# A hybrid decoder layer on one core: another opening stage, a second exponential buffer in GLA, weight low halves in four parts

## What is computed

```python
h = rmsnorm(x, g_mix)
q_g, k_g, v_g, r_g, a_low, q_d, k_d, v_d, q_i, k_i, w_i, gate_g, gate_d = split(h @ w_in)
k_i = layernorm(k_i)
log_a = log_sigmoid(a_low @ w_gate_up + b_gate) / 16
o_g, s_new = gla_chunked(q_g, k_g, v_g, log_a, state)        # 4 heads, dk 128, dv 256
o_g = rmsnorm(o_g) * silu(r_g)
# DSA: indexer scores of 4 heads pick the top 256 causal keys of each query
score[t, s] = sum_h w_i[t, h] * relu(q_i[t, h] . k_i[s])
o_d = softmax(q_d . k_d + bias, over the picked keys) @ v_d   # 8 heads of 64
x = x + (sigmoid(gate_g) * (o_g @ w_gla) + sigmoid(gate_d) * (o_d @ w_dsa)) @ w_o
x = x + swiglu(rmsnorm(x, g_ffn));  y = rmsnorm(x, g_final)
```

## Time and profile before

| | |
|---|---|
| median of three runs | 2203.22 us (2202.76 to 2204.34) |
| profiled execution, its span | 2211.91 us, 2210.2 us |
| TensorE busy | 2096.9 us, 95% of the span |
| VectorE, ScalarE, GpSimd busy | 1072.6, 627.2, 334.7 us |
| mean granted clock of TensorE | 0.963 |

### The profile page before, as it was taken

One profiled execution on the slowest core, in us unless ns is written; L12 is line 12 of the kernel. 1 busy time (PEld: TensorE's weight loads), 2 busy tenths in 40 slices (PEclk: granted clock), 3 DMA queues, 4 the chain that ended last, 5 costly groups with the idle time before them and its releaser, 6 DMA issues. The chain is left out here.

```text
span 2210.2 us, 31133 instructions
## 1 busy us (share of the span) xinstructions
PE 2096.9 (95%) x12125; PEld 1873.6 (85%) x12125; DVE 1072.6 (49%) x2226; ACT 627.2 (28%) x1108; POOL 334.7 (15%) x294
## 2 busy tenths in 40 slices
PE   5999996999999999988889999999999999999997
PEld 4789996999999786777759987888998899889995
DVE  5489997345454330545554424444334432443245
ACT  4323221223333361444344313311212111111112
POOL 6512222333223121001013310000000000000000
PEclk7999998999999899998979999999999999999999
DMA  4202331222212242343344340211011110111002
GB/s 139 85 20 77 118 107 59 87 78 80 67 58 83 64 134 88 131 140 144 124 159 151 117 144 1 77 58 39 29 48 58 39 52 26 58 58 39 20 1 89
DMA packets 144139, 173.82 MB, mean 79 GB/s; under 512 B 9688, under 2 KB 120830, under 8 KB 143486
## 3 DMA queue, kind: packets, MB, share of 16 engines
q1 hardware_dynamic: 136158, 148.14, 20.6%
q0 software_dynamic: 7840, 23.67, 3.1%
HBM read 127.38 MB, written 44.40 MB: 78 GB/s over the span
## 5 line engine op out<-in xcount | busy, mean ns | idle before, releaser
L855 PE MATMUL ring<-n_hi,piece_hi 128*128 128x352 f32 (+1 forms) x1320 | 441.4, 334 | 1.1 <-DVE n_whole L1664 1.0
L857 PE MATMUL ring<-n_hi,piece_lo 128*128 128x352 f32 (+1 forms) x1320 | 429.5, 325 | 0.0
L856 PE MATMUL ring<-n_lo,piece_hi 128*128 128x352 f32 (+1 forms) x1320 | 429.1, 325 | 0.0
L1241 ACT ACTIVATE arena<-ring 128x352 f32<-128x352 f32 (+7 forms) x368 | 153.3, 438 | 483.6 <-PE ring L857 345.3
L2198 POOL TENSOR_TENSOR piece_lo<-piece_whole,piece_hi 128x1024 fp32r<-128x1024 f32 (+2 forms) x71 | 165.5, 2331 | 714.1 <-ACT piece_hi L1254 714.0
L855 PEld LDWEIGHTS ring<-n_hi,piece_hi 128*128 128x128 f32 (+1 forms) x1320 | 251.8, 191 | 9.0 <-issue 6.7
L856 PEld LDWEIGHTS ring<-n_lo,piece_hi 128*128 128x128 f32 (+1 forms) x1320 | 252.3, 191 | 0.6
L857 PEld LDWEIGHTS ring<-n_hi,piece_lo 128*128 128x128 f32 (+1 forms) x1320 | 251.2, 190 | 0.5
L1752 DVE TENSOR_SCALAR_CACHE_REDUCE arena<-arena 128x384 uint8<-128x384 f32 (+6 forms) x224 | 190.7, 875 | 1.4 <-DVE arena L1752 0.2
L856 PE MATMUL ring<-h_lo,gate_hi 128*128 128x352 f32 x528 | 170.7, 323 | 6.2 <-issue 6.2
L855 PE MATMUL ring<-h_hi,gate_hi 128*128 128x352 f32 x528 | 172.0, 326 | 0.0
(11 more groups left out here) (278 smaller groups left out, 3679.0 us busy)
## 6 DMA issues: line engine op xcount, KB each, us to landing
piece_whole<-w_in SPq DMA_DIRECT2D x54, 512.0 KB, 3.6
projected_rows<-arena SPq DMA_DIRECT2D x44, 528.0 KB, 2.7
arena<-projected_rows SPq DMA_DIRECT2D x12, 1056.0 KB, 5.0
gate_whole<-w_ffn_gate SPq DMA_DIRECT2D x11, 1024.0 KB, 5.2
up_whole<-w_ffn_up SPq DMA_DIRECT2D x11, 1024.0 KB, 5.3
down_whole<-w_ffn_down SPq DMA_DIRECT2D x11, 1024.0 KB, 4.7
arena<-projected_rows SPq DMA_DIRECT2D x16, 528.0 KB, 3.6
arena<-x_prompt SPq DMA_DIRECT2D x16, 512.0 KB, 5.2
```

The costliest lines, as they stand in the source:

```text
L855: pe.matmul(out, lhi, rhi, start=first, stop=False)
L856: pe.matmul(out, lhi, rlo, start=False, stop=False)
L857: return pe.matmul(out, llo, rhi, start=False, stop=last)
L1241: evacuates(act.activation(dst, src, ACT.Copy, scale=scale), *key)
```

## The change

The norm weight is laid out over all partitions (`grow`) and applied with the scaling, before the tiles are turned. The high part is copied by ScalarE and the low part subtracted by VectorE, both out of PSUM; GpSimd has no part in it. Each tile has its own buffer. The loads are issued in another order: the fourth tile stands behind the first weight loads. Six groups of pieces 0 and 1 and the page transposes run among the tiles' transposes. Pages are loaded with one DMA each instead of two, from the start on. The scores go over heads 0 and 1 of all blocks first, then 2 and 3; two groups of piece 2, the sample scores (with another order of their matmuls) and their sums are inside the list. The bias rows move behind piece 3's groups, their shift from VectorE to ScalarE. Low halves of pieces 5 to 23 are made in four instructions of 128x256. In GLA the second and fourth exponential have a buffer of their own, `eT2`, in place of `k4p`; their order in the chain changes; the next head's first difference is made before the outputs are gated, and all rows are scaled before the first is gated.

```diff
+        def early_groups(i):
+
+            return {3: [(0, 0)], 5: [(1, 0)], 6: [(0, 1)], 8: [(1, 1), (0, 2), (1, 2)]}.get(i, [])
+        def nb_after(n, g):
+            return range(4 * g, 4 * g + 4) if n == 3 and g < 2 else []
...
-        SCC = [(b, h, c0, min(512, P * (b + 1) - c0)) for b in range(2, NTP)
-               for c0 in range(0, P * (b + 1), 512) for h in range(IH)]
+        SCC = [(b, h, c0, min(512, P * (b + 1) - c0)) for f in range(2) for b in range(2, NTP)
+               for c0 in range(0, P * (b + 1), 512) for h in (2 * f, 2 * f + 1)]
+        HALF = len(SCC) // 2
+
+        def score_groups(n):
+
+            return {6: [(2, 0)], 13: [(2, 1)]}.get(n, [])
...
-        xa = [arena[:, B_kd + i * D:B_kd + (i + 1) * D] for i in range(4)]
+        xa = [arena[:, o:o + D] for o in [B_kd + i * D for i in range(4)] + [B_SC + i * D for i in range(4)] + [B_nb]]
         sqj = arena[:, B_vd:B_vd + D]
...
+        grow = arena[:, B_vd + D:B_vd + 2 * D]
...
+        eT2 = at(o_k4p, T)
...
-            sp.dma_start(arena[:, o_c128:o_c128 + n128], a["c128"]).then_inc(c_first, 16)
+            sp.dma_start(arena[:, o_c128:o_c128 + P], a["c128"][:, 0:P]).then_inc(c_first, 16)
+            load_x(0)
+            sp.dma_start(grow, a["g_mix"].to_broadcast([P, D])).then_inc(grow_in, 16)
...
+            sp.dma_start(relb[0:NB, :], a["rel_bias"]).then_inc(relb_in, 16)
+            load_x(1)
+            sp.dma_start(pagetab[0:1, :], a["page_table"].rearrange("(o b) g -> o (b g)", o=1)).then_inc(pagetab_in, 16)
+            load_x(2)
+            load(0)
+            load_x(3)
+            load_x(4)
+            load(1)
+            for i in range(5, NT):
+                load_x(i)
...
+                    for c0, cn in ((0, PAST), (PAST, DT)):
+                        for hp in range(2):
+                            for j in range(4):
+                                b = 4 * g + j
+                                rhs = kiS[:, b, :] if c0 == 0 else kiT[:, SEQ + b * DT:SEQ + (b + 1) * DT]
+                                ins = pe.matmul(ps[32 * j:32 * j + 32, c0:c0 + cn], qiS[:, 2 * b + hp, :], rhs,
+                                                start=hp == 0, stop=hp == 1)
+                    done(ins, "si", g)
...
+                for n, g in early_groups(i):
+                    if n == 0:
+                        for k in range((3 * g), min(NT, 3 * g + 3)):
+                            for c in range(2):
+                                wait_evac(pe, "h", k, c)
+                    dense(n, g)
+                    if (n, g) == (1, 1):
+                        pe.wait_ge(pg_landed, 16 * DB * NPG)
+                        for k in range(4):
+                            transposes(("ps", k), [(P * s, kpg[:, 4 * k + s, :]) for s in range(4)])
...
+            for n, (b, h, c0, w_) in enumerate(SCC):
+                for m in score_groups(n):
+                    dense(*m)
+                if n == HALF:
+                    for m in range(3):
+                        wait_evac(pe, "d", 2, m)
+                    sample_scores()
+                if n == HALF + 6:
+                    sample_sums()
...
+                    wait_full(act, "h", i, c)
+                    act.activation(n_hi[:, 4 * c:4 * c + 4, i * P:i * P + r],
+                                   bank("h", i, c).rearrange("p (a b) -> p a b", a=4)[:, :, 0:r],
...
+            square_x(0)
+            square_x(1)
+            root_x(0)
             act.wait_ge(c_first, 16 * N_FIRST)
             copy_out(vec, bank("vec")[:, 0:22], "vec")
-            for i in range(NT + 3):
...
+            square_x(2)
+            root_x(1)
+            norm_hi(0)
+            square_x(3)
+            root_x(2)
+            norm_hi(1)
+            hi_piece(0)
+            square_x(4)
+            root_x(3)
+            norm_hi(2)
+            hi_piece(1)
+            square_x(5)
+            root_x(4)
+            norm_hi(3)
+            square_x(6)
+            root_x(5)
+            square_x(7)
+            first_out(0, 0)
+            norm_hi(4)
+            root_x(6)
+            norm_hi(5)
+            square_x(8)
+            root_x(7)
+            first_out(1, 0)
+            norm_hi(6)
+            root_x(8)
+            first_out(0, 1)
+            norm_hi(7)
+            norm_hi(8)
+            first_out(1, 1)
+            for n in range(4):
+                copy_out(kiS[:, 2 * n:2 * n + 2, :], bank("ps", n).rearrange("p (a b) -> p a b", a=2), "ps", n)
+            first_out(0, 2)
+            hi_piece(2)
+            first_out(1, 2)
...
+                    for h in nb_after(n, g):
+                        if h == 0:
+                            wait_full(act, "sc", *SCC[-1])
+                            act.wait_ge(qis_done, 1)
+                        wait_full(act, "nb", h)
+                        link(act.activation(r31[:, h:h + 1], bank("nb", h)[:, 0:1], ACT.Copy, scale=-1.0))
+                        if h >= 4:
+                            act.wait_ge(nb_out[h % 4], 16)
+                        evacuates(act.activation(nbs[h % 4], bank("nb", h)[:, 0:383], ACT.Identity,
+                                                 bias=r31[:, h:h + 1]), "nb", h)
...
-                act.wait_ge(d_done, 5 * h + m + 1)
-                if m >= 1:
-                    act.wait_ge(f_done, 5 * h + m)
-                if m == 2:
...
+
+                if m == 0:
+                    act.wait_ge(d_done, 3 * h + 1)
+                    act.wait_ge(f_done, 5 * h)
+                    ins = act.activation(eT, dT, ACT.Exp, scale=1 / 16)
+                elif m == 1:
+                    if h == 0:
+                        act.wait_ge(od_out, 16 * (NTP + 1))
+                    ins = act.activation(eT2, dT, ACT.Exp, scale=-1 / 16)
+                elif m == 2:
+                    act.wait_ge(f_done, 5 * h + 1)
+                    ins = act.activation(eT, uB[:, h, :], ACT.Exp, scale=1 / 16)
+                elif m == 3:
+                    act.wait_ge(f_done, 5 * h + 2)
+                    act.wait_ge(d_done, 3 * h + 2)
+                    act.activation(c128_(eT2)[:, :, 0:64], c128_(dT)[:, :, 0:64], ACT.Exp, scale=-1 / 16)
+                    ins = act.activation(c128_(eT2)[:, :, 64:P], c128_(dT)[:, :, 64:P], ACT.Exp, scale=1 / 16)
                 else:
-                    act.activation(eT, uB[:, h, :] if m == 3 else dT, ACT.Exp,
-                                   scale=(1 / 16, -1 / 16, 0, 1 / 16, -1 / 16)[m]).then_inc(e_done, 1)
+                    act.wait_ge(f_done, 5 * h + 3)
+                    act.wait_ge(d_done, 3 * h + 3)
+                    ins = act.activation(eT, dT, ACT.Exp, scale=-1 / 16)
+                ins.then_inc(e_done, 1)
...
+            def norm_input(i):
+                r = rows(i)
+                v.wait_ge(x_rt, i + 1)
+                link(v.reciprocal(rstd[0:r, i:i + 1], rt[0:r, i:i + 1]))
+                v.scalar_tensor_tensor(xa[i][0:r, :], xa[i][0:r, :], rstd[0:r, i:i + 1], grow[0:r, :],
+                                       ALU.mult, ALU.mult).then_inc(x_h, 1)
+            def split_input(i):
                 r = rows(i)
                 for c in range(2):
+                    at_ = (slice(None), slice(4 * c, 4 * c + 4), slice(i * P, i * P + r))
                     wait_full(v, "h", i, c)
-                    if i >= 2:
-                        v.wait_ge(n_lo_done, 2 * (i - 2) + c + 1)
-                    g = vec[:, 4 * c:4 * c + 4].unsqueeze(2).to_broadcast([P, 4, r])
+                    v.wait_ge(n_hi_done, 2 * i + c + 1)
                     src = bank("h", i, c).rearrange("p (a b) -> p a b", a=4)[:, :, 0:r]
-                    evacuates(v.tensor_tensor(ht[(2 * i + c) % 4][:, :, 0:r], src, g, ALU.mult), "h", i, c)
+                    evacuates(v.tensor_tensor(n_lo[at_], src, n_hi[at_], ALU.subtract), "h", i, c)
...
+                if n == HALF:
+                    sample_weights()
+                if n == HALF + 2:
+                    weigh_sample()
+                if n == HALF + 8:
+                    sample_rows()
...
+            def chain_start(h):
+                Bc = uB[:, h, :]
+                mid = c64(Bc)[:, :, 31:32].to_broadcast([P, 16, 64])
+                v.tensor_tensor(c64(dT), c64(Bc), mid, ALU.subtract)
+                link(v.tensor_copy(dT[:, SEQ:T], Bc[:, SEQ:T]))
+                v.sem_inc(d_done, 1)
...
+                for i in range(NT):
+                    r = rows(i)
+                    row = vh[:, i, :] if i < NTP else o8[0:r, :]
+                    v.tensor_scalar(row, row, ors[0:r, i:i + 1], None, ALU.mult).then_inc(on_done, 1)
+                if h + 1 < GH:
+                    chain_start(h + 1)
+                for k in range(NT):
...
+                    evacuates(v.tensor_tensor(out, src, mine, ALU.mult), "gt", h, k)
...
-                g.tensor_tensor(lo, raw, hi, ALU.subtract).then_inc(p_lo_done, 1)
-
...
-            for i in range(NT):
-                r = rows(i)
```

(27 more changed lines are left out.)

366 lines of the change are left out of this document (157 added, 209 removed).

## The result

The changed kernel takes 2156.95 us, median of 4 runs (2155.36 to 2158.77), against 2203.78 us in runs of the kernel before on the same chip. The ratio is 0.9786, 95% interval [0.9774, 0.9799]: faster by 46.8 us. The prediction was 2143, with a range of 2124 to 2172; the time lies inside the range and 14 us above the forecast.

What follows compares the result with a forecast made beforehand. TensorE was taken as the bound, with long waits in the opening, before attention and in the GLA heads. Attention 37.5 us earlier plus 22.5 in heads made 60: 2211.9 to 2152 profiled, 2143 us median, range 2124 to 2172.

Steps and rivals of the forecast that it cites:

- The opening to the first score: Opening: without GpSimd's tail, TensorE's queue sets the pace; first score at 68.5 us against 93.0, ends 61 and 82.
- rival 1: Opening: TensorE stays at 1.2 GHz, first score at 82 to 90, attention 17 to 20 us later, 2162; chance 0.14.
- The scores: Score stage before the search: 37.5 us against 37.8, with two projection groups and the sample scores now inside it.
- ring and two buffers cover some 3.2 of VectorE's work: Scores: a group keeps TensorE away 3.8 us, buffered work covers 3.2; 2.5 us each taken, 5 for two.
- The four parts: Top-k search: low halves in four GpSimd instructions shorten VectorE's holds, 15 us saved; ends 24 saved and 22 lost.
- Rivals 3: Search: each of four parts is paid whole, search 264.5 us, attention only 3 us earlier, 2177; chance 0.06.
- 4: Search: parts of 1.2 us, each paid whole, search 302 us, kernel slower at 2215; chance 0.03.
- TensorE's road: Projection groups up to attention: 232.5 us from a start at 103.5, ending at 336, last by 2 us.
- two roads to attention: Start of attention: VectorE's search ends at 334, TensorE's projection groups at 336; attention 37.5 us earlier.
- The heads: GLA heads: second buffer and early first difference gain 22.5 us, 15 of waits and 7.5 of clock; ends 10 and 32.
- Rival 2: GLA heads: something else holds TensorE or the clock still falls; only 5 of 22.5 us come, 2160; chance 0.14.
- From the profiled execution to the median: Whole kernel: the profiled execution's 8.7 us over the median carried over in full, turning 2152 into 2143.

Runs made afterwards that it cites:

- experiment 1: Changed kernel with each low half of the weight pieces made in one GpSimd instruction, as before the change; ratio 0.9793 to the kernel before.
- experiment 2: Changed kernel with GpSimd's preparation of the first attention masks moved ahead of the last weight pieces; ratio 0.9767 to the kernel before.
- experiment 10: Changed kernel with 40 needless GpSimd memsets ahead of the first attention masks, to delay attention; ratio 0.9871 to the kernel before.
- experiment 7: Changed kernel with the two projection groups between score tiles moved ahead of the scores; ratio 0.9755 to the kernel before.
- experiment 6: Changed kernel, second exponential buffer kept, but early first difference and separate scaling and gating loops undone; ratio 0.9814 to the kernel before.
- experiment 4: Kernel before with only the low halves of the search's weight pieces made in four GpSimd instructions; ratio 0.9972 to the kernel before.
- experiment 5: Kernel before with only the new GLA heads (second buffer, early chain start, separate scaling loop); ratio 0.9872 to the kernel before.
- experiment 11: Kernel before with low halves in four parts and the new GLA heads, without the new opening; ratio 0.9833 to the kernel before.
- experiment 9: Changed kernel with the sample-score matmuls in their old order (batch, columns, head pair); ratio 0.9836 to the kernel before.

## Why the prediction was right, and where it was off

The direction, the mechanisms and the places held; the profiled time (2155) was forecast at 2152 and the median (2157) at 2143. Point by point:

- **The opening to the first score: held, 2 us late.** 70.5 for the first ScalarE operation of the scores against 68.5. TensorE ran at full clock through 20 to 40 us in the changed kernel's trace, and at 0.84 to 0.89 in those of experiments 1, 2 and 10, which have the same opening; the 0.5 of rival 1 is out. VectorE's two-input norm was held beside GpSimd's two weight pieces: 2.50 (18.65) and 1.95 us (22.51) instead of 1.28, 1.9 in all. The rule of the Trainium skill ("SBUF — State Buffer", "Who interferes with whom") that spoke against this edit is borne out by these two lines, at half the 3.6 us that it would give at most; TensorE's early groups covered it.
- **The scores: 46.2 instead of 37.5, the term that failed most.** The two groups were sized at 5 us (ends 2 and 10); experiment 7 shows 9.9. The step that failed is the cover, "ring and two buffers cover some 3.2 of VectorE's work": it was 2.1 us at the first group. The step missed that TensorE has nothing for 6.5 us in the layer norm just before, so that the score matmuls ahead of the group run at half clock and are hardly ahead of VectorE. The size is that of the upper end, but not for the reason given with it: the groups themselves ran at full clock. Another 1.6 us is the hold at 87.30 by the low halves of piece 4, which are made whole; it is in experiment 7, too. The sample scores lie within the bounds, 2.1 us a half-batch, but the stall was put at 1.5 us and VectorE's gap behind them is 3.83, at a granted clock of 0.50 (2.62 in experiment 7). Of the 8.7 us by which the stage is longer than forecast some 1 us is not accounted for.
- **The four parts: held, better than sized.** The search took 221.6 us against 241.4 in before and 238.7 in experiment 1: 17 to 20 us, forecast 15. No small operation in the rows shown is near the 2.27 us of the earlier trace rows; their mean is 0.24 to 0.30 us. Rivals 3 and 4 are out.
- **TensorE's road: 232.4 against 232.5**, from a start 10.0 us later than forecast (113.5 against 103.5), since the scores ended later.
- **What is late next: missed.** The prediction had two roads to attention and compared them to 2 us. There was a third, GpSimd's queue, which the row of 361.19 in the earlier trace rows showed: masks made behind the last piece, under the 16.7 us of TensorE's wait. It cost 7.0 us. Experiment 2 takes 5.2 of them back. So attention came 20.6 us earlier: 37.5, less 9.9 for TensorE's later end, less 7.0.
- **The heads: 34, not 22.5.** The waits were right (15 forecast; 13.5 by the wait rows, 15.5 of idle time in all). The clock was mis-sized: 7.5 forecast, 18.4 measured as busy time of the same matmuls. The step took one stretch (902 to 936, clock 0.90) and allowed 3.4 us a head at the most; over the whole stage, up to the output projection, the clock was 0.92, and after the change 0.97. Part of the 18.4 may be luck of the execution: the four traces with the old heads are alike (373 to 374 us busy), but those with the new ones have 355 to 358 or 364 to 365, so the gain was 9 us in two of them. The loops, taken at nothing, and the early start bring back 6 us by ratio when undone together (experiment 6), hardly more than the uncertainty, and 2 us of waits. Rival 2 is out.
- **From the profiled execution to the median: failed.** The prediction carried 8.7 us over in full ("nothing in these stages is of that"). The profiled execution of before stood 8 us above its median; that of after stands 1.6 below. So 56.5 us by the profiles are 46.8 by the medians. Part of it can be seen: with the same opening code the search started at 131.1 in it, and at 128.8, 130.0 and 130.2 in experiments 4, 5 and 11; its attention started 3.7 us later than in experiment 5, which has the same code up to there; and the changed kernel's stretch from the gate logits to the first head was some 3 us shorter than in nearly all others. The gains read from one pair of profiles held some 10 us of luck.

By the traces the two misses cancel in part, 16.9 us lost at attention and 11.4 won in the heads, so the forecast of the profiled time is off by 3 us only; that closeness is luck. The rest of the 14 us is the last point.

## What to carry to other kernels

Before you say which of two roads comes last, list every engine that the waiting instruction needs, and how far each is behind its cover: the wait that you remove was also hiding the others (here GpSimd's masks, 6.7 us, of which their order in the queue gave 5.2 back). Put independent groups where TensorE would stand idle ahead of a chain of small steps, not between the steps: the two groups cost 9.9 us between score tiles and nothing ahead of them, where they also kept the clock up. When you price short waits of TensorE, sum the busy time of the same matmuls over the whole stage; in these heads the clock brought 18.4 us and the waits 15.5, though in two other traces the clock brought only some 9. Trace a kernel more than once before you build on a gain of that size.

## What the runs showed of the hardware that was not expected

- The same 2146 matmuls with the same waits were busy for 355 us in one kernel and 365 in another, at mean granted clocks of 0.97 and 0.94, in code that the kernels share (experiments 5 and 9 against the changed kernel). Whether it is the kernel or the single execution isn't shown. A difference of 10 us between two traces can come from such a stage alone, so an edit's worth is to be read at its own place first.
- A VectorE operation held beside GpSimd's work in four parts is freed within a part: 186 small operations lost 17 us less in all than beside whole pieces, for 0.4 us more of GpSimd's time a piece (2.8 against 2.4).
- The order in which small matmuls are issued decides: a half-batch of the sample scores took 2.10 us at a granted clock of 0.50 where four matmuls in a row write four different ranges of 32 partitions, and 3.83 us at 1.00 where four in a row write the same range (experiment 9).
- A subtraction over 1024 columns (two instructions of 512), one operand in PSUM, and a two-operand norm in SBUF both took 1.28 us; only the second was held by GpSimd's pieces (2.50 and 1.95; the subtraction between them at 21.07, which begins while piece 20.86 runs, took 1.27).
